# A two-block network on one core: group norm in one PSUM bank, ada products inside the scan, two more homes for split weights, and a last norm about a shifted mean

## The reference

```python
def step(S, inp):                        # 8 heads of 64, 512 steps
    S = S * w_t[:, :, None, :] + sa[..., None] * b_t[:, :, None, :] + v_t[..., None] * k_t[:, :, None, :]
    y = jnp.einsum("bhvk,bhk->bhv", S, r_t)
...
y = ((y - mu) * lax.rsqrt(var + GN_EPS)).reshape(B, T, H * N)      # mean and variance over a head's 64
y = y * g + b
rwkv_out = (y + bonus.reshape(B, T, D_RWKV)) * g_gate
c = jax.nn.silu(_layer_norm(_causal_dwconv(c, ...), cln_g, cln_b))
mix = jnp.concatenate([rwkv_out, c], axis=-1) @ w_out
...
m = jax.nn.silu(cvec) @ w + b                                      # adaln
...
x = layer_norm(DEEPNORM_ALPHA * x + gate[:, None, :] * (o @ out_w[i]), ln_g[i], ln_b[i])
```

## Time and profile before

| What | us |
|---|---|
| Median of 3 runs | 1906.13 (1905.41 to 1911.1) |
| The profiled execution | 1912.22 |
| Its span in the profile | 1910.4 |
| PE, DVE, POOL, ACT busy | 1785.0, 1032.5, 950.6, 753.4 |

### The profile page before, as it was taken

The page is one execution under the profiler, slowest core; times in us unless marked ns, Lnnn a source line. Parts: engine busy times, 40 slices in busy tenths (PEclk is TensorE's granted clock), DMA queues, the critical chain, the costliest instruction groups (busy, mean ns, idle before and its releaser), DMA issues.

```text
span 1910.4 us, 24095 instructions
## 1 busy us (share of the span) xinstructions
PE 1785.0 (93%) x9352; PEld 1407.6 (74%) x9352; DVE 1032.5 (54%) x1224; ACT 753.4 (39%) x1219; POOL 950.6 (50%) x754
## 2 busy tenths in 40 slices
PE   4999999988999999999898899999988999999976
PEld 1677999865668888887587677776846888888764
DVE  4398454247465555200544667666565566666564
ACT  3452667213233333100322555555134444444433
POOL 3354677700749999989245321224623444444071
PEclk8899999799999999999999999999998999999988
DMA  4121000205202222322311100002130111111111
GB/s 177 45 89 67 1 1 1 111 1 198 88 24 108 88 103 95 135 107 88 121 67 45 44 23 1 23 1 88 67 134 31 45 45 57 54 45 45 67 67 44
DMA packets 18572, 126.15 MB, mean 66 GB/s; under 512 B 2064, under 2 KB 2064, under 8 KB 4016
## 3 DMA queue, kind: packets, MB, share of 16 engines
q1 hardware_dynamic: 17904, 121.72, 17.3%
q10 hardware_dynamic: 576, 3.15, 0.5%
HBM read 122.76 MB, written 2.10 MB: 65 GB/s over the span
## 4 chain that ended last, share of the span: by engine, by line
PE 49%; issue 22%; POOL 16%; DVE 8%; ACT 3%; DMA 1%; POOLq 0%; SPq 0%; ACTq 0%; DVEq 0%
POOL w_hi L587 8%; PE banks L1075 4%; POOL cacc L611 4%; POOL w_lo L579 4%; PE banks L1202 3%; PE banks L1054 3%; PE banks L1205 3%; PE banks L1203 3%; PE banks L936 3%; PE banks L941 2%; PE banks L937 2%; PE banks L1257 2%; PE banks L668 2%; PE banks L670 2%; PE banks L669 2%
## 5 line engine op out<-in xcount | busy, mean ns | idle before, releaser
L587 POOL TENSOR_TENSOR w_hi<-raw,der 128x512 fp32r<-128x512 f32 x300 | 347.0, 1167 | 593.9 <-PE banks L1205 211.6
L579 POOL TENSOR_TENSOR w_lo<-raw,w_hi 128x512 fp32r<-128x512 f32 x336 | 470.2, 1412 | 75.8 <-ACT w_hi L1330 75.8
L668 PE MATMUL banks<-h_hi,w_hi 128*128 128x512 f32 x592 | 236.6, 400 | 18.8 <-DVE h_lo L1893 13.1
L670 PE MATMUL banks<-h_hi,w_lo 128*128 128x512 f32 x592 | 232.1, 392 | 0.0
L669 PE MATMUL banks<-h_lo,w_hi 128*128 128x512 f32 x592 | 232.1, 392 | 0.0
L1202 PE MATMUL banks<-h_hi,w_hi 128*128 128x512 f32 (+1 forms) x384 | 147.4, 384 | 4.4 <-DVE h_lo L2358 3.6
L668 PEld LDWEIGHTS banks<-h_hi,w_hi 128*128 128x128 f32 x592 | 112.1, 189 | 52.0 <-issue 15.5
L1203 PE MATMUL banks<-h_lo,w_hi 128*128 128x512 f32 (+1 forms) x384 | 131.5, 357 | 0.0
L669 PEld LDWEIGHTS banks<-h_lo,w_hi 128*128 128x128 f32 x592 | 112.3, 190 | 23.4 <-issue 1.2
L670 PEld LDWEIGHTS banks<-h_hi,w_lo 128*128 128x128 f32 x592 | 112.1, 189 | 23.7
L1805 ACT ACTIVATE dP<-banks,der 128x768 f32<-128x768 f32 x64 | 57.7, 902 | 166.6 <-DVE der L2391 166.6
(11 more groups left out here) (418 smaller groups left out, 4127.3 us busy)
## 6 DMA issues: line engine op xcount, KB each, us to landing
raw<-in_stream SPq DMA_DIRECT2D x84, 1024.0 KB, 4.8
ada_raw<-in_ada_w SPq DMA_DIRECT2D x20, 1024.0 KB, 5.4
raw<-in_ada_w SPq DMA_DIRECT2D x4, 1024.0 KB, 4.7
xT<-in_x_t SPq DMA_DIRECT2D x2, 1024.0 KB, 6.3
xT<-in_x_t SPq DMA_DIRECT2D x1, 2048.0 KB, 9.3
out_t<-z SPq DMA_DIRECT2D x8, 256.0 KB, 2.1
ctxT<-in_ctx_t ACTq DMA_DIRECT2D x1, 1024.0 KB, 4.7
rope<-in_ropes ACTq DMA_DIRECT2D x2, 512.0 KB, 3.6
```

What stands on the lines that cost most here:

```text
L579: return pool.tensor_tensor(w_lo[:, half, part(i), :], raw_tiles(half)[:, part(i), :], w_hi[:, half, part(i), :], ALU.subtract)
L587: pool.tensor_tensor(w_hi[:, half, part(i), :], raw_tiles(half)[:, part(i), :], one, ALU.mult).then_inc(hi_done, 1)
L668: pe.matmul(banks[b][:, :], hi, rhs_hi[:, k, :], start=(at_k == 0), stop=False)
L670: mm = pe.matmul(banks[b][:, :], lo, rhs_hi[:, k, :], start=False, stop=(at_k == KT - 1))
```

## The change

In the scan PE no longer brings the state into the bank by the identity. DVE multiplies the old state by the decay into the new buffer while PE works, and then adds the bank times the decay in eight pieces of 64x64. Ada blocks 0 to 5 follow chunks 1 to 6; the first two lie in the halves of `raw`, so the output blocks 11 and 12 load only after them. DVE's `ada_columns` stand in chunks 3, 5 and 7, and the reciprocal and multiply of the convolution's norm move one chunk earlier.

In the group norm the four variances go to 32 rows each of one bank, one root and one reciprocal serve all heads, and four products with the new constant `spread` bring the result to the full tiles. Gain and gate are one DVE instruction; bonus and gate are multiplied on GpSimd. The first four output tiles are accumulated together, one input tile after the other. The third and fourth output blocks have homes of their own (`w3`, `w4`), and the two blocks of the next stage are split under the projection.

In the last norm ACT scales the input ahead of time, DVE takes each tile directly from PSUM and adds in one instruction. After four tiles the mean of these is taken as a shift of all; the squares are summed about it. The variance is made per token with one-column sums (mean of squares less square of the mean), its reciprocal root is spread to all partitions by four products, and meanwhile DVE takes off the rest of the mean.

```diff
+        def weights_behind(n, b):
+            sp.wait_ge(*(ada_pair(b // 2) if b % 2 else (ada_free, b // 2 + 1)))
+            sp.dma_start(raw[:, half_of(n), :], stream[n, :, :]).then_inc(raw_full[half_of(n)], 16)
+        out0 = STREAM["out"]
+        weights(0, out0)
+        for b in range(2):
+            sp.wait_ge(split_full, out0 + b - 1)
+            ada_block(b)
         for e in range(2):
             sp.wait_ge(u_pe[e], len(PE_STEPS) * CT)
-        for b in range(3):
-            ada_block(b)
-        sp.wait_ge(conv_done, len(ADDED))
+        sp.dma_start(spread[:, :], squares[:, 8, :]).then_inc(s_const, 16)
+        ada_block(2)
         ada_block(3)
-        weights(STREAM["out"] + 2, STREAM["out"] + 3)
-        sp.wait_ge(y_full, NCH)
-        ada_block(4, 0)
+        weights_behind(out0, 0)
+        weights_behind(out0 + 1, 1)
+        weights(out0 + 2, out0 + 3)
+        ada_block(4, 2)
+        weights(out0 + 3, out0 + 4)
+        ada_block(5, 3)
...
+        ada_block(6, 4)
+        sp.wait_ge(gn_spread, CT)
+        ada_block(7, 5)
+        weights(STREAM["up"], STREAM["up"] + 2)
+        sp.wait_ge(block_done, out0 + 3)
         ada_block(8, 4)
-        ada_block(7, 4)
-        sp.wait_ge(gn_normed, CT)
         ada_block(9, 5)
-        weights(STREAM["up"], STREAM["down"] + 4)
+        weights(STREAM["up"] + 2, STREAM["down"] + 4)
...
+        split(out0 + 2, half_of(out0 + 2), out0 // 2 + 1, done=out0, to=0, hi=w3_hi, lo=w3_lo)
+        pool.wait_ge(*bonus_shifted.at(CT))
+        for c in range(CT):
+            pool.tensor_tensor(rr[:, c, :], rr[:, c, :], gg[:, c, :], ALU.mult).then_inc(bonus_gated.sem, 1)
+        for c in range(CT):
+            pool.wait_ge(gn_centred, c + 1)
+            pool.wait_ge(*bonus_gated.at(c + 1))
+            pool.tensor_tensor(gg[:, c, :], gg[:, c, :], ky[:, c, :], ALU.mult).then_inc(y_gated.sem, 1)
+        split(out0 + 3, half_of(out0 + 3), (out0 + 3) // 2, done=out0, to=0, hi=w4_hi, lo=w4_lo)
+        split(out0 + 4, half_of(out0 + 4), (out0 + 4) // 2, done=out0 + 1)
+        split(out0 + 5, half_of(out0 + 5), (out0 + 5) // 2, done=out0 + 2)
+        split(out0 + 6, half_of(out0 + 6), (out0 + 6) // 2)
...
-            if n < NCH - 1:
-                for c in range(CT):
-                    pe.matmul(banks[1][:, P * c:P * c + P], ident, state[:, c, :], start=(c == 0), stop=False, skip_group_check=True)
...
+            if n == 1:
+                pe.wait_ge(silu_c, 1)
+            if 1 <= n < NCH - 1:
+                ada_blocks([n - 1])
...
+        OUT_ORDER = [4, 5, 6, 7, 0, 1, 2, 3]
+        def out_tile(m, k):
+            hi, lo = OUT_W[m // 2]
+            t = KT * (m % 2) + k
+            b = banks[OUT_BANK[m]]
+            pe.matmul(b[:, :], hi[:, t, :], h1_hi[:, k, :], start=(k == OUT_ORDER[0]), stop=False)
+            pe.matmul(b[:, :], hi[:, t, :], h1_lo[:, k, :], start=False, stop=False)
+            mm = pe.matmul(b[:, :], lo[:, t, :], h1_hi[:, k, :], start=False, stop=(k == OUT_ORDER[-1]))
+            if k == OUT_ORDER[-1]:
+                mm.then_inc(tile0_full if m % 2 == 0 else block_done, 1)
...
+        def conv_tiles(k):
+            pe.wait_ge(mix_ready, k - CT + 1)
+            for m in range(4):
+                out_tile(m, k)
...
-            pe.matmul(banks[GN_BANK[c]][:, :], head_ones, ky[:, c, :], start=True, stop=True).then_inc(gn_mean, 1)
+            pe.matmul(banks[4 + c][:, :], head_ones, ky[:, c, :], start=True, stop=True).then_inc(gn_mean, 1)
         for c in range(CT):
+            pe.wait_ge(gn_centred, 1)
             pe.wait_ge(gn_sq, c + 1)
-            pe.matmul(banks[GN_BANK[c]][:, :], head_ones, msq[:, c % 2, :], start=True, stop=True).then_inc(gn_var, 1)
-        for n in range(STREAM["out"], STREAM["out"] + N_OUT):
-            project([2 * s, 2 * s + 1], s, n, n // 2 + 1, h1_hi, h1_lo, ready=mix_ready if n == STREAM["out"] else None,
-                    order=[both_parts(k) for k in range(KT)], between=((1, 2), (3,), (4,), (5,)) if n == STREAM["out"] else ())
+            pe.matmul(banks[4][32 * c:32 * c + 32, :], head_ones[:, 48:80], msq[:, c % 2, :], start=True, stop=True).then_inc(gn_var, 1)
+        for n in (out0, out0 + 1):
+            pe.wait_ge(split_full, n + 1)
+            for j in range(2):
+                pe.wait_ge(proj_free[2 * half_of(n) + j], n // 2 + 1)
+        conv_tiles(4)
+        conv_tiles(5)
+        pe.wait_ge(gn_inverse, 1)
+        pe.wait_ge(s_const, 112)
+        for c in range(CT):
+            rows = slice(32 * c, 32 * c + 32)
+            pe.matmul(banks[SPREAD_BANK[c]][:, :], spread[rows, :], mrs[rows, :], start=True, stop=True).then_inc(gn_spread, 1)
+        conv_tiles(6)
+        conv_tiles(7)
+        for m in range(4):
+            for k in range(CT):
+                if m == 0:
+                    pe.wait_ge(mix_ready, CT + k + 1)
+                out_tile(m, k)
...
+        for m in range(4, KT):
+            if m % 2 == 0:
+                pe.wait_ge(split_full, out0 + m // 2 + 1)
+            for k in OUT_ORDER:
+                out_tile(m, k)
...
+        def last_norm():
+            z7 = z1[:, KT - 1, :]
+            pe.wait_ge(z_acc, KT + 5)
+            pe.matmul(banks[5][:, :], ones, zacc[:, 0:T], start=True, stop=False)
+            token_sums(3, zacc, True, False)
+            pe.wait_ge(*u_sq_added.at(6))
+            token_sums(6, qacc, True, False)
+            pe.wait_ge(z_centred, 2 * KT)
+            pe.matmul(banks[5][:, :], ones, z7, start=False, stop=True).then_inc(z_sum, 1)
+            token_sums(3, z7, False, True).then_inc(z_sum, 1)
+            pe.wait_ge(z_sq, 2 * KT)
+            token_sums(6, usq[:, 3, :], False, True).then_inc(z_sum, 1)
+            pe.wait_ge(*token_root.at(2))
+            for j in range(4):
+                mm = pe.matmul(banks[7][:, P * j:P * j + P], der[:, TOK + 8 + j:TOK + 9 + j].broadcast_to([P, P]), ident, start=True, stop=True)
+            mm.then_inc(z_sum, 1)
...
+                if layer and m == 4:
+                    product(m, range(4))
+                    pe.wait_ge(z_acc, KT + 3)
+                    pe.matmul(banks[4][:, :], ones, zacc[:, 0:T], start=True, stop=True).then_inc(z_sum, 1)
+                    product(m, range(4, KT))
...
+                for e in range(2):
+                    hr = slice(64 * e, 64 * e + 64)
+                    decay = der[hr, ECT:ECT + 32].rearrange("p (c n) -> p c n", n=NCH)[:, :, n + 1:n + 2].broadcast_to([64, CT, 64])
+                    ins = dve.tensor_tensor(St[(n + 1) % 2][hr, :, hr], St[n % 2][hr, :, hr], decay, ALU.mult)
+                chain.link(ins)
                 dve.wait_ge(st_full, n + 1)
                 for e in range(2):
                     hr = slice(64 * e, 64 * e + 64)
-                    src = banks[1][hr, :].rearrange("p (c v) -> p c v", c=CT)[:, :, hr]
-                    decay = der[hr, ECT:ECT + 32].rearrange("p (c n) -> p c n", n=NCH)[:, :, n + 1:n + 2].broadcast_to([64, CT, 64])
-                    dve.tensor_tensor(St[(n + 1) % 2][hr, :, hr], src, decay, ALU.mult).then_inc(st_done, 1)
+                    for c in range(CT):
+                        kept = St[(n + 1) % 2][hr, c, hr]
+                        at_decay = ECT + NCH * c + n + 1
+                        ins = dve.scalar_tensor_tensor(out=kept, in0=banks[1][hr, P * c + 64 * e:P * c + 64 * e + 64],
+                                                       scalar=der[hr, at_decay:at_decay + 1], in1=kept, op0=ALU.mult, op1=ALU.add)
+                    ins.then_inc(st_done, 1)
...
+            if n in (3, 5, 7):
+                ada_columns((n - 3) // 2)
...
+        dve.wait_ge(gn_root, 1)
+        dve.reciprocal(mrs[:, :], mrs[:, :]).then_inc(gn_inverse, 1)
...
+            dve.wait_ge(gn_spread, c + 1)
+            dve.wait_ge(*y_gated.at(c + 1))
+            chain.link(dve.scalar_tensor_tensor(out=ky[:, c, :], in0=banks[SPREAD_BANK[c]][:, :], scalar=col("lnx_g", c), in1=gg[:, c, :],
+                                                op0=ALU.mult, op1=ALU.mult))
+            dve.tensor_tensor(ky[:, c, :], ky[:, c, :], rr[:, c, :], ALU.add).then_inc(mix_full, 1)
+            if c:
+                mix_low(c - 1)
+        mix_low(CT - 1)
...
+        for m in range(4):
+            take(m, z_gated)
+            if m:
+                add_tile(m, m - 1)
+        dve.wait_ge(z_sum, 10)
+        for m in range(4, KT):
+            dve.wait_ge(*u_scaled.at(m + 1))
+            shift(z[:, m, 0:T])
+            if m == 4:
+                for k in range(4):
+                    shift(z1[:, k, :], z_centred)
+        chain.wait()
+        for k in range(1, 4):
+            add_square(k)
+        take(4, z_centred)
+        add_square(4)
+        for m in (5, 6):
+            take(m, z_centred)
+            add_tile(m, m - 2)
+            add_square(m)
+        take(7, z_centred)
...
+        dve.wait_ge(z_sum, 11)
+        for k in range(2):
+            centre(k)
```

(15 more changed lines are left out.)

189 lines of the change are left out of this document (121 added, 68 removed).

## The result

The changed kernel takes 1883.39 us (median of 4 runs, 1880.98 to 1889.05) where the kernel before takes 1908.62 (4 runs, 1905.41 to 1915.58): ratio 0.9852, 95% interval 0.9819 to 0.9884. Predicted were 1883.0 us, a range of 1876 to 1894 and faster with 0.94.

A forecast was written before the change was run, and what follows sets the result against it. PE bounds it, at half clock early in the scan; DVE sets the pace in the group norm. Up to the projection -18.5 plus 1.5 given back is -17.0; last norm -6.3; total -23.3 from 1906.13: 1883 us, range 1876 to 1894.

The forecast's parts named there:

- Identity products: Scan: gone from seven chunks, 1.04 us each in five at full clock, some 1.95 in two at half: -9.1.
- DVE's updates: Scan: eight 64x64 state updates taken as 1.7 us, between 0.88 and 3.5; +0.65 in chunk 0.
- The wait for SA in chunk 6: Scan: reciprocal and columns together in chunk 5 make PE wait, +1.7; 1.5 given back for low clock behind new waits.
- rival 1: Scan and group norm: DVE falls behind beside GpSimd, gain 9.8 us smaller at 13.5, 1893 us; chance 0.17.
- Waits of the group norm: Between 437 and 465: waits of 2.34 + 2.80 us go, -5.1, and their half-clock shares, -3.4.
- Spread products: Group norm: four new products of 512 columns each, at 3.70/4 us: +3.6.
- Slack of about 1 us at two places: Group norm into projection: PE stays fed; DVE ends the normed tiles at 456, PE wants the fourth at 457.
- Weights and queues: Scan and projection: ada blocks 4 and 5 land near 405 and 415, wanted at 416 and 425; splits in time.
- rival 3: Scan: the clock does not rise with the ada blocks, 46.7 us more, 1930 us, slower; chance 0.04.
- The splits of the next stage under the projection: Priced at nothing: two blocks were split before the next stage's inputs were ready too.
- Last norm: End of kernel: tail 27.15 to 18.7, -8.45; one sum of 0.9 and a stall of 1.2 added: -6.3.
- Rival 2: Last norm gives nothing: DVE holds the buffers, PE stalls 2 us each at fifth to seventh tiles; 1889 us; chance 0.08.

The follow-up runs named there:

- the second set: The changed kernel once more, unedited, in six further runs beside 17 of the kernel before: 1887.37 us, ratio 0.9862.
- e5: Changed kernel with the identity products on PE again and DVE's state update in two instructions: 1891.49 us, ratio 0.9897 to the kernel before.
- e7: Changed kernel with the convolution norm's sums of squares behind chunk 3 and their reciprocal in chunk 4: 1882.5 us, ratio 0.9844 to the kernel before.
- e9: Changed kernel with GpSimd's split of the fourth out block only after the mixer's last low part: 1884.94 us, ratio 0.986 to the kernel before.
- e10: As e7, with GpSimd's split of the fourth out block late: 1883.67 us, ratio 0.9861 to the kernel before.
- e6: Changed kernel with all four spread products on rows 0 to 31 instead of four groups: 1890.83 us, ratio 0.9886 to the kernel before.
- e11: As e8, with GpSimd's split of the fourth out block late: 1879.97 us, ratio 0.9838 to the kernel before.
- e4: Changed kernel with the next stage's two splits late, beside the post norm again: 1889.62 us, ratio 0.988 to the kernel before.
- e8: As e7, with the third ada columns moved behind the last addition of y: 1879.33 us, ratio 0.9841 to the kernel before.

## Why the prediction was right, and where its terms were not

The mechanism held: what was taken from PE's path in the mixer and in the last norm is gone at the places named, by -15.2 and -1.8 us for -17.0, and by -7.2 for -6.3. That the median came out at 1883.39 for 1883.0 is partly luck: the median of the second set is 1887.37, several terms were off in ways that cancel, and 1.8 of the mixer's 17.0 us came from a step priced at nothing. One sign that the prediction named as "wrong" did appear, a granted clock under 0.9 after 385: it is 0.80 from 420 to 432 and 0.88 from 432 to 440.

- *Identity products, -9.1.* Gone; e5 shows 0.95 us a chunk at full clock (9.16 less 8.21). Over the five chunks at full clock it was taken back, all or nearly all of it, by the wait and the clock that it uncovered, so in this kernel the term was worth something mainly in the first two chunks.
- *DVE's updates, 1.7 us.* Measured 1.79, and chunk 0 waits 0.90, predicted 0.65.
- *The wait for SA in chunk 6, +1.7, with 1.5 given back to the clock.* The place and the cause (columns and reciprocal in one chunk) were right. The wait is 2.38, since DVE's decays took 2.77 us beside GpSimd; the clock behind it cost more as well. The prediction has 3.2 us for this wait and for the clock behind both remaining waits. By e7 this wait and the clock behind it cost 3.7, and the slow means another 1.7; the term for the clock, 1.5, is the most undersized one, at 3.3. The part of the wait beyond 1.7 is rival 1's mechanism (DVE beside GpSimd): about 0.7 us here and 0.8 at the normed tiles (e9, e10), of the 9.8 it was given.
- *Waits of the group norm, -5.1 and -3.4.* Gone as said, by the traces; no run put the old order back. New is 0.86 us for ACT's squares, which the prediction had not asked for.
- *Spread products, +3.6.* The mis-sized term: 1.14 us, by e6 because they stand on four groups of rows. The first two products of the variances, into two groups of 32 output rows, took 1.05 us where the earlier trace rows gives 1.85, but the second two 1.54; that this is the same effect was not tested.
- *Slack of about 1 us at two places.* One was missed by 1.03: PE was there 2.5 us sooner than worked out, and DVE's additions took 1.12 and 1.01 beside the split; e9 to e11 take 0.5 of the wait away.
- *The four sums ahead of the rise of the clock* took 6.18 us, in the earlier trace rows 5.15; the prediction left them alone. Without the identity products they come sooner in the low spell.
- *Weights and queues.* No wait of PE for an ada or out block in the scan; rival 3 (clock does not rise) did not happen, windows from 378 to 418 show 1.00.
- *Sum.* -17.0 predicted for the stretch, -15.1 measured (151.28 to 136.15). "The splits of the next stage under the projection are worth nothing" was wrong: -1.8, shown by e4. The argument (both blocks were ready in time before too) was about GpSimd's result; the gain lies in what DVE does while GpSimd works. The misses of the stretch partly cancel, by rows of this case. Up to the means 10.6 us are gone instead of 13.6 (with the five ada blocks that moved counted in at 3.64 us each, and without the 1.5 given back): the four sums cost 1.0, the SA wait 0.7, chunk 0's wait 0.2 and the slow ada block with its neighbour 1.6 more, and 0.5 came from an SA wait at 391.39 in the kernel before that the prediction did not count. Behind that 4.6 are gone instead of 4.9: slow means 1.7, the missed slack 1.0 and the squares 0.9 against 2.5 from the spread products and 1.2 from the variances.
- *Last norm, -6.3.* Tail 18.12 for 18.7; sum and wait 1.02 and 0.80 for 0.9 and 1.2; net -7.2 by the marks. The six steps on PE add up to 5.8 in the prediction, not 5.9; they took 5.34 (1860.92 to 1866.26). A group of one-column sums took 0.95 to 1.03 us, 0.81 to 0.89 from start to start, against the 1.04 of four 128-column products: near the upper bound that was chosen. Its reason, that the loads of weights are the same, was not tested. Rival 2 (two-us stalls at the fifth to seventh tile) did not happen.

The rule weighed in the prediction can be read again. In e8 and e11 the same addition of two SBUF operands takes 1.47 us beside the split and 0.69 without it, while the multiply that reads one operand from PSUM takes 0.74 in both. The Trainium skill, "SBUF — State Buffer", section "Who interferes with whom", states that of these two only the first contends with a GpSimd instruction that reads SBUF. The multiply reads a second tile from SBUF beside its PSUM input, and stays at 0.74: the trace agrees.

What stays open: the group norm's new order, the largest single term, and the ada blocks inside the scan have no run of their own and rest on the two traces; what makes the clock fall at 70 to 80 us in some executions and not in others; why it was low behind the spread products of e5 and e6, and at the means in some traces and not in others; and how large the last norm's gain is as a time, since the part between the post norm's root and PE's last product alone ran from 1372.5 to 1376.0 us over the traces with the new last norm.

## What to carry to other kernels

Removing work from the engine that sets the pace is worth only what its feeder can follow (in the five chunks of e5, taking 4.75 us of products away gained 0.7 us at most): list per round what the feeder has to do, put its two longest items into different rounds, and count them at the price they have beside the engine that slows them. Moving a bulk job away from the short additions that it slows (here GpSimd's splits away from DVE's last sum) is worth something even when its result was never waited for. And where executions differ by more than the effect, compare marks inside the traces, after checking that code which did not change takes the same time in both, and start the count behind the place where the two executions part.

## What the runs showed of the hardware that was not expected

Four products of 32 rows and 512 columns in fp32, each on its own group of 32 rows and into its own bank, took 1.14 us together; on one group of rows 4.29, at a granted clock of 0.87. Eight records of 128 rows take 3.70 at full clock, 3.2 times as much. The Trainium skill, "TensorE: Matmul & The Clock Gate", section "Part 3: Packing small matmuls — row/col tiling", gives a measured speedup of 3.07 for four products of 32 rows and 512 columns; the trace is near it. Two products with 32 output rows each, into different groups of rows of one bank, took 1.05 us, against 1.85 for two of 128; the next two took 1.54.

Two decays of 64x256 with both operands in SBUF took 0.84 us alone and 2.77 beside GpSimd, 3.3 times, more than the 1.66 for 0.69 of the earlier trace rows.

A wait of PE of 1.90 us ahead of the post norm's sum left that sum at 1.13 us in nine traces of ten (1.85 in e6); a wait of 2.7 to 2.8 us was followed by 2.07 or 2.08 in four of four. Behind the wait of 2.23 us in the old last norm the same kind of sum took 1.12 us in one trace and 1.88 in another. And one stretch of unchanged code (70 to 80 us) ran at 0.50 to 0.62 of the full clock in eight of fourteen traces and at 1.00 in six, which moved everything behind it by about 5 us.
